# Attention's copies, norms and square roots in another order on ScalarE and the vector engine

## What is computed

```python
def diff_attn_core(q, k, v, lam):
    s = jnp.einsum('bqhid,bkhid->bhiqk', q, k) * (HEAD_DIM ** -0.5)
    p = jax.nn.softmax(s.astype(jnp.float32), axis=-1)
    a = p[:, :, 0] - lam * p[:, :, 1]
    return jnp.einsum('bhqk,bkhe->bqhe', a.astype(v.dtype), v)
...
def diff_head_out(o, subln_gain, lam_init, w_o):
    o = rmsnorm(o, subln_gain) * (1.0 - lam_init)
    return o.reshape(o.shape[0], o.shape[1], V_WIDTH) @ w_o
```

## Time and profile before

| | |
|---|---|
| median of 3 runs | 2561.04 us |
| the profiled execution: its time | 2561.38 us |
| its span (first to last instruction) | 2559.7 us |
| what lies around the span | 1.7 us |
| TensorE busy | 98% of the span |
| VectorE, ScalarE, GpSimd busy | 80%, 50%, 8% |
| mean granted TensorE clock | 0.996 |

### The profile page before, as it was taken

One profiled execution on the slowest core, in us unless ns is written; L12 is line 12 of the kernel. 1 busy time (PEld: TensorE's weight loads), 2 busy tenths in 40 slices (PEclk: granted clock), 3 DMA queues, 4 the chain that ended last, 5 costly groups with the idle time before them and its releaser, 6 DMA issues.

```text
span 2559.7 us, 39781 instructions
## 1 busy us (share of the span) xinstructions
PE 2508.8 (98%) x14322; PEld 2179.4 (85%) x14322; DVE 2056.5 (80%) x2729; ACT 1275.3 (50%) x1730; POOL 198.1 (8%) x301
## 2 busy tenths in 40 slices
PE   6999999998999999999999999999999999999998
PEld 3778888777888888888888988888988888888887
DVE  6888887887898889987888799989988877775443
ACT  5422334676565555555444544445655555554443
POOL 1002221000000001100111011101000000000000
PEclk9999999999999999999999999999999999999999
DMA  9768887554778778887999699978688766655553
GB/s 352 272 221 267 302 268 227 165 157 140 239 245 273 255 256 270 287 263 228 296 293 296 221 318 329 333 230 273 211 280 269 253 189 189 188 191 186 187 188 135
DMA packets 465214, 623.53 MB, mean 244 GB/s; under 512 B 18804, under 2 KB 404246, under 8 KB 458160
## 3 DMA queue, kind: packets, MB, share of 16 engines
q1 hardware_dynamic: 424544, 450.94, 53.0%
q0 software_dynamic: 40208, 170.51, 20.3%
q10 hardware_dynamic: 320, 0.13, 0.0%
HBM read 619.41 MB, written 2.10 MB: 243 GB/s over the span
## 4 chain that ended last, share of the span: by engine, by line
PE 83%; DVE 8%; ACT 4%; DMA 3%; issue 2%; SPq 0%; ACTq 0%; DVEq 0%; POOLq 0%
PE ps L1923 49%; PE ps L1931 26%; DVE w_lo L1130 2%; PE ps L1846 2%; DMA raw<-in_sconv_w_in_dram 2%; PE ps L1848 1%; PE ps L1847 1%; ACT w_hi L622 1%; DVE ada_sum L1201 1%; DVE start_sum L1124 1%; DMA raw<-in_ffn_w_up_dram 1%; DVE ada_sum_b L1201 1%; DMA first_x<-in_w_ada_dram 1%; PE ps L2064 0%; PE ps L2046 0%
## 5 line engine op out<-in xcount | busy, mean ns | idle before, releaser
L622 ACT ACTIVATE w_hi<-raw 128x1024 fp32r<-128x1024 f32 (+1 forms) x800 | 821.7, 1039 | 903.6 <-PE ps L1931 451.8
L1130 DVE TENSOR_TENSOR w_lo<-raw,w_hi 128x1024 fp32r<-128x1024 f32 (+1 forms) x800 | 955.2, 1201 | 389.4 <-ACT w_hi L622 386.6
L1923 PE MATMUL ps<-xs,w_hi 128*128 128x512 f32 x3200 | 764.3, 393 | 0.7 <-DVE v_rows L1178 0.5
L1923 PEld LDWEIGHTS ps<-xs,w_hi 128*128 128x128 f32 x3200 | 592.8, 188 | 125.6 <-issue 6.6
L1931 PEld LDWEIGHTS ps<-xs,w_lo 128*128 128x128 f32 x3200 | 403.4, 191 | 11.6 <-DVE w_lo L1130 0.8
L1931 PE MATMUL ps<-xs,w_lo 128*128 128x256 f32 x3200 | 409.4, 283 | 0.6 <-DVE w_lo L1130 0.6
L1923 PE MATMUL ps<-act,w_hi 128*128 128x512 f32 x1408 | 331.4, 391 | 0.0
L1923 PEld LDWEIGHTS ps<-act,w_hi 128*128 128x128 f32 x1408 | 260.5, 188 | 51.8
L1931 PEld LDWEIGHTS ps<-act,w_lo 128*128 128x128 f32 x1408 | 175.4, 191 | 3.8
L1931 PE MATMUL ps<-act,w_lo 128*128 128x256 f32 x1408 | 177.1, 283 | 0.0
L1923 PE MATMUL ps<-xs_sin,w_hi 128*128 128x512 f32 x704 | 170.2, 392 | 0.6 <-DVE xs_sin L1374 0.5
(11 more groups left out here) (258 smaller groups left out, 2765.6 us busy)
## 6 DMA issues: line engine op xcount, KB each, us to landing
raw<-in_ffn_w_up_dram SPq DMA_DIRECT2D x352, 512.0 KB, 4.6
ada_ring<-in_w_ada_dram POOLq DMA_DIRECT2D x176, 512.0 KB, 5.1
raw<-in_ffn_w_down_dram SPq DMA_DIRECT2D x128, 512.0 KB, 4.4
raw<-in_attn_w_qkv_dram SPq DMA_DIRECT2D x96, 512.0 KB, 4.8
broad_ring<-in_w_ada_dram POOLq DMA_DIRECT2D x48, 1024.0 KB, 5.9
raw<-in_sconv_w_in_dram SPq DMA_DIRECT2D x96, 512.0 KB, 5.7
ada_ring_kv<-in_w_ada_dram POOLq DMA_DIRECT2D x48, 512.0 KB, 5.0
raw<-in_ffn_w_down_dram SPq DMA_DIRECT2D x64, 384.0 KB, 3.4
```

The lines of the kernel that those rows point to most:

```text
L622: nc.scalar.activation(w_hi[:, slot, 0:n_tiles, :], raw[:, slot, 0:n_tiles, :], ACT.Copy).then_inc(hi_made, 1)
L1130: nc.vector.tensor_tensor(w_lo[:, slot, 0:n_tiles, :], raw[:, slot, 0:n_tiles, :], w_hi[:, slot, 0:n_tiles, :], ALU.subtract).then_inc(lo_ ...
L1923: last = mm(ps[:, bank + m, :], w_hi[:, slot, t, P * m:P * m + P], src[:, tile + t, :], start=(is_first and t == 0), stop=(is_last and t = ...
```

## The change

On ScalarE, `keep_a(h, 0)` and `gain(h-2)` are taken out of the attention point and put ahead of `hi` of the same unit, in a function `early_point`. After each `root` of a head below 6 one Exp of a single column of ones follows, and after the last exponentials one Sqrt; nobody reads their results. At the end of attention both engines take the steps of heads 6 and 7 in another order, and o's first eviction moves ahead of the last two copies of x. No instruction changes otherwise: TensorE, GpSimd and the DMA queue keep their programs.

```diff
             def root(h):
                 se.wait_ge(o_inverted, h + 1)
                 nc.scalar.activation(o_rstd[:, :, bass.ds(h, 1)], o_inv[:, :, bass.ds(h, 1)], ACT.Sqrt).then_inc(o_root, 1)
+                if not isinstance(h, int) or h < 6:
+                    nc.scalar.activation(lam_exp[:, 0:1], ones[:, 0:1], ACT.Exp)
...
                 if k == 2 and at(0):
+                    exponentials(h, 1)
+                if k == 3 and at(-1):
+                    square_o(h + (-1), 1 - parity)
+
+            def early_point(k, h):
+
+                at = lambda m: not isinstance(h, int) or 0 <= h + m < HEADS
+                if k == 2 and at(0):
                     keep_a(h, 0)
-                    exponentials(h, 1)
-                if k == 3:
-                    if at(-2):
-                        gain(h + (-2))
-                    if at(-1):
-                        square_o(h + (-1), 1 - parity)
+                if k == 3 and at(-2):
+                    gain(h + (-2))
 
             def q_pair(i):
                 for h in range(2):
                     for k in range(4):
+                        early_point(k, 2 * i + (h - 2))
                         hi(2 * i + (UNITS["q"] // 4 + h), k)
...
             o_hi_unit(4)
+            early_point(2, 7)
             attention_point(2, 7, 1)
+            nc.scalar.activation(lam_exp[:, 1:2], ones[:, 0:1], ACT.Sqrt)
+            early_point(3, 7)
             attention_point(3, 7, 1)
             o_hi_unit(5)
             attention_point(0, 8, 0)
+            root(6)
             keep_x(0, 1)
-            attention_point(1, 8, 0)
             o_hi_unit(6)
-            attention_point(3, 8, 0)
-            attention_point(1, 9, 1)
+            square_o(7, 1)
+            gain(6)
+            root(7)
             o_hi_unit(7)
-            attention_point(3, 9, 1)
-            keep_x(2, 3, 4, 5, 6, 7)
+            gain(7)
+            keep_x(2, 3, 4, 5)
+            res_point(2, "o", 0, 0, RES["o"])
+            keep_x(6, 7)
...
@@ the vector engine
             attention_point(3, 7, 1)
+            invert(6)
             o_lo_unit(5)
-            attention_point(0, 8, 0)
-            attention_point(1, 8, 0)
-            attention_point(2, 8, 0)
+            scale_o(6, 0)
+            keep_o(7, 1, 1)
             o_lo_unit(6)
-            attention_point(3, 8, 0)
-            attention_point(0, 9, 1)
-            attention_point(1, 9, 1)
+            invert(7)
+            scale_o(7, 1)
+            low_o(6)
             o_lo_unit(7)
-            attention_point(3, 9, 1)
-
+            low_o(7)
+
+            ve.wait_ge(xt_kept, 1)
+            res_point(2, "o", 0, 0, B0 + G1)
             ve.wait_ge(xt_kept, 8)
```

More of the change, by code:

```diff
@@ L883, in _ @@
             for k in range(4):
+                early_point(k, 6)
                 o_hi_unit(k)
@@ L911, in o_pair @@
                         hi(2 * i + (UNITS["o"] // 4 + h), k)
-                        if isinstance(i, int) and h == 0 and k < 2:
-                            res_point(k + 2, "o", 0, 0, RES["o"])
+                        if isinstance(i, int) and h == 0 and k == 1:
+                            res_point(3, "o", 0, 0, RES["o"])
                         res_point(k, "o", 2 * i + (h - 1), 1 - h, RES["o"])
@@ L1589, in o_pair @@
                         lo(2 * i + (UNITS["o"] // 4 + h), k)
-                        if i == 1 and h == 0 and k < 2:
-                            res_point(k + 2, "o", 0, 0, B0 + G1)
+                        if i == 1 and h == 0 and k == 1:
+                            res_point(3, "o", 0, 0, B0 + G1)
                         n = 8 * i + 4 * h + k - 8
```

## The result

The changed kernel takes 2567.57 us (median of eight runs, 2565.05 to 2570.02), the kernel before on the same chip 2560.02 us (2557.30 to 2561.94): a ratio of 1.0030 with a 95% interval of 1.0021 to 1.0038, or 7.5 us more. The profiled execution took 2567.88 us with a span of 2566.2, 6.5 us more than that of before.

A forecast was written before the change was run, and what follows sets the result against it. TensorE, busy for 98% of the span, was taken to bound the kernel. Terms 8.0 + 1.1 - 2.4 + 3.1 = +9.8 us gave 2570.8 us on the median (2571.2 on the profiled execution); range 2563 to 2576.

The forecast's parts named there:

- The row behind the copy: Heads 0 to 5, `turn_a(h, 0)` to `turn_a(h, 1)`: work behind the copy to `a_t` takes 11.76 us; +8.0 us.
- The first link: Start of `turn_a(h, 0)` to the copy to `a_t`: the turn, 0.60, and 0.04 to the next engine; 0.64 us.
- The way back: From `turn_a(h, 1)` to `turn_a(h+1, 0)`: TensorE's own work, staying at 9.48 us.
- The Exp: After each root: table load now ahead of the copy, nothing in heads 2 to 5, +1.1 us in head 6.
- Gain ahead of `w_hi`: Unit 3: three gain instructions delay `w_hi`, covered by TensorE's turn and next scores; costed at nothing.
- The end of attention: Heads 6, 7 and o's third slab: waits shrink, 2.97 us won, 0.6 charged for two loads; -2.4 us.
- The clock: Behind eight waits in attention: lower clock after the long one and one of seven others, 1.55 us each; +3.1 us.
- rival 1: In attention: the copy still ties the row to the turn, but the clock doesn't fall; 6.7 us, 2567.7; chance 0.17.
- Rival 4: Heads: the copy's wait goes, nothing replaces it; 4.5 us won there, 3.0 at the end, 2553.5; chance 0.07.
- rival 3: Heads: the row behind the copy has 0.7 us more slack a head, no further clock fall; 2563.5; chance 0.11.
- Rival 5: ScalarE's table switches ahead of the copy, heads 2 to 6: each drains 1.38 us on top; 2585 us; chance 0.01.

The follow-up runs named there:

- e8: The changed kernel with ScalarE making `w_hi` of unit 3 twice in the eight slabs of the q projection: 2569.93 us, ratio 1.0040.
- e1: The kernel before with only `keep_a(h, 0)` moved ahead of unit 2's `w_hi` in every head: 2569.61 us, ratio 1.0039.
- e3: The kernel before with only `gain(h-2)` moved ahead of unit 3's `w_hi`: 2561.21 us, ratio 1.0003.
- e4: The kernel before with only the new order at the end of attention, including the early Sqrt table: 2556.56 us, ratio 0.9985.
- e7: The changed kernel with ScalarE making `w_hi` of unit 2 twice in the eight slabs of the q projection: 2578.55 us, ratio 1.0080.
- e2: The kernel before with only an Exp of one column added behind each root of heads 0 to 5: 2563.88 us, ratio 1.0014.
- e5: The kernel before with the new end of attention and `keep_a(h, 0)` of heads 0 to 6 between `copy_a` and `rotate`: 2553.23 us, ratio 0.9972.

## Why the prediction held, point by point

**The row behind the copy** (forecast 11.76 us, +8.0 for heads 0 to 5): right in its mechanism. Each link is in the traces; the sum measured 11.61 us and +7.1. Two links were charged too long: the adaLN piece ends its part after 1.45 us (550.17 to 551.62), not 1.53, since the next instruction starts before it has ended, and from the reciprocal to the last step it is 0.96 (551.62 to 552.58), not 1.10. The first link was 0.72 and not 0.64. That isn't the two loads ahead of the copy, which end just in time (542.46): where ScalarE idles in front of the copy, as in head 4 of e8, it starts at T + 0.71 too. The way back was 9.53, as in the rows of before (9.48).

**The Exp.** For head 6 13.2 us were forecast and 13.00 came, and a wait near 5.5 was 5.26. At nothing a head the price in heads 2 to 5 was about right, but only because the copy stands behind it: alone the Exp costs 3.4 us, and on top of the better order 5.4. The reason that it doesn't pay is one link of the prediction's list: beside the sine product, the sum and the adaLN piece (548.84 to 551.62, 2.8 us) the exponentials (548.83 on, 1.4 us) are early anyhow. Even a load of 1.28 us in front of them fits in: e1 has it there (547.74), and its reciprocal starts 9.85 us behind the turn (540.69 to 550.54), that of the changed kernel 9.84. The drain of 1.38 us that the Trainium skill gives for each switch ("ScalarE: Activation LUTs", section "What ACT_TABLE_LOAD costs") isn't in these traces: the load lasts 1.28 us, starts 0.01 to 0.02 us behind the root (540.95 to 540.97) and is followed by the Exp 0.01 us later.

**Gain ahead of `w_hi`:** nothing, as forecast; e3 shows no difference.

**The end of attention** (-2.4 forecast): 37.60 us less 1.37 lost by the clock is 36.2, so -3.2. The 0.6 us charged for the two loads ahead of unit 4's `w_hi` was mis-sized; 0.27 us on `a_t` is all that shows. And head 7's `turn_o` has no wait at all, where 0.2 was left to it. Alone the new end gave 4.0 us.

**The clock** (+3.1 forecast): this is the term that was most off. The wait of 5.26 us was followed by 3.42 us at 0.60, 3.42 x 0.40 = 1.4 us; none of the seven waits of 1.1 to 1.9 us was, where I had counted one. The rate of 1.55 us a fall was right within 0.2 where TensorE's own work follows. It is less where another wait follows: the fall of before slowed `weigh(6, 0)` by 1.55 us, but `turn_a(6, 0)` to `turn_a(6, 1)` took only 0.5 us more than in e3 and e4, which have no fall there (12.08 for 11.60), since the next wait shrank from 2.13 to 0.93 us. The number of falls was taken from one case, the 1.86 us before `weigh(6, 0)`, and e3 and e4 have the same wait of 1.86 us with the clock at 1.00 behind it.

By the profile that makes 7.1 + 0.9 - 3.2 + 1.4 = +6.2, and 0.3 ahead of attention. The forecast had +9.8; it was too high by 0.9 for the row, 0.2 for the Exp, 0.8 for the end and 1.7 for the clock. The result, 2567.57, lies on rival 1 (2567.7), but by luck: that rival is the same mechanism without a fall of the clock, and the clock did fall once. Its other terms sum to +6.7, and the profile has +4.8 for them. Rival 4 fails with e1, rival 3 with the list of waits and with e7: the row has no slack. Rival 5 fails with the rows of the table loads.

## What to carry to other kernels

On an engine that takes its instructions in order, an instruction that waits for another engine is an anchor: moved forward, it ties all that it passes to that wait. Before moving it, sum the row from it to the next wait of the bounding engine, and compare with that engine's own work between the two points; here 11.6 us stood against 9.9. A better place is a gap in which its engine waits already and its data is ready (1.74 us here): the move to the front cost 9.1 us, the move into the gap gave 2.3 us beyond the 4.0 of the new end, and it took 9.0 us off the changed kernel.

## What the runs showed of the hardware

The granted clock behind a wait of TensorE isn't set by the wait's length alone. In these traces of attention it stayed at 1.00 behind all 30 waits from 1.1 to 1.64 us, behind seven of eight from 1.80 to 1.91 us, and behind both of 2.13 us. Behind both of 1.99 us, behind five of six from 2.29 to 2.85 us and behind all seven of 3.39 us and more it was 0.50 to 0.67 over the 3.4 us that followed, so for most of them at the lower of its two levels, 1.2 GHz. Those of 3.39 us and more are all in head 6. Shorter waits weren't counted; one of 0.93 us, in e2, has 0.50 behind it because the clock hadn't risen again since the wait of 3.39 us, 5.6 us earlier. The clearest pair is the wait of 1.86 us on `a_t` in head 6, which three kernels have alike: before with 0.54 behind it, e3 and e4 with 1.00. Ahead of it TensorE did the same in all three: a wait of 1.33 to 1.38 us, then some 5.2 us of work. What else decides wasn't settled. The runs of one kernel spread over 5 us and more. Falls that come and go fit that, but weren't shown to be the cause, and the up to 2.9 us by which the part behind the third slab differs between traces have another cause, which wasn't found: in six of the traces (before, changed, e4, e5, e7, e8) every 5 us of the 1920 us behind it have a granted clock of 1.00. A fall cost 1.4 us in the changed kernel and 1.7 in e7 and e8 (11.2 for 9.53 us on the way back). It is easily missed: in e7 a step of 1.05 us more a head cost 1.1 by itself and in most heads another 1.7 by the clock.
